# Two feed-forward layers in Strassen form: sums and low parts moved to VectorE, modulation products to ScalarE

## The reference, cut to what matters

```python
# first block, its end
x = x + rms_norm(mixed, mix_post_norm)
h = rms_norm(x, ffn_pre_norm)
f = jnp.square(jax.nn.relu(h @ w_up)) @ w_down        # 1024 -> 4096 -> 1024
x = x + rms_norm(f, ffn_post_norm)
# second block
mod = c @ w_ada + b_ada                               # 1024 -> 6 * 1024: shifts, scales, gates
...
h2 = modulate(rms_norm_2(x, g_pre_mlp), sh2, sc2)
ff = jnp.square(jax.nn.relu(h2 @ w_mlp_in)) @ w_mlp_out
x = x + gt2 * rms_norm_2(ff, g_post_mlp)
```

## Time and profile before

| | |
|---|---|
| median of three executions | 3071.1 us (3069.76 to 3072.03) |
| profiled execution, its own time | 3071.47 us |
| span of its trace, first to last instruction | 3069.7 us |
| mean granted TensorE clock | 0.953 of full speed |
| TensorE (PE) busy | 2753.1 us (90% of the span) |
| VectorE (DVE) busy | 1730.3 us (56%) |
| GpSimd (POOL) busy | 1597.4 us (52%) |
| ScalarE (ACT) busy | 1030.7 us (34%) |
| entry, up and down of run 0 | about 700 to 1523 us of the span |
| entry, up and down of run 1 | about 2280 to 3057 us |

### The profile page before, as it was taken

One profiled execution on the slowest core, in us unless ns is written; L12 is line 12 of the kernel. 1 busy time (PEld: TensorE's weight loads), 2 busy tenths in 40 slices (PEclk: granted clock), 3 DMA queues, 4 the chain that ended last, 5 costly groups with the idle time before them and its releaser, 6 DMA issues. The chain is left out here.

```text
span 3069.7 us, 39464 instructions
## 1 busy us (share of the span) xinstructions
PE 2753.1 (90%) x15794; PEld 2218.5 (72%) x15794; DVE 1730.3 (56%) x1707; ACT 1030.7 (34%) x1748; POOL 1597.4 (52%) x930
## 2 busy tenths in 40 slices
PE   7999998978899887898799999988996999978897
PEld 6887567866777666777678887656875888757775
DVE  3465544653799986776743003674144333367767
ACT  3324663325432322222420003553035333322322
POOL 4321002447688857877732322112364777678876
PEclk9999999989899998999999999999997999989999
DMA  3210000032355553223321111001133233422132
GB/s 123 55 27 16 10 1 23 3 117 96 103 185 158 184 189 116 88 75 110 110 70 50 52 35 35 14 8 49 48 138 117 76 110 110 175 100 88 62 110 110
DMA packets 219188, 256.80 MB, mean 84 GB/s; under 512 B 16119, under 2 KB 157710, under 8 KB 219022
## 3 DMA queue, kind: packets, MB, share of 16 engines
q1 hardware_dynamic: 206494, 210.97, 21.1%
q10 hardware_dynamic: 12528, 43.52, 3.7%
HBM read 204.13 MB, written 50.33 MB: 83 GB/s over the span
## 5 line engine op out<-in xcount | busy, mean ns | idle before, releaser
L369 POOL TENSOR_SCALAR slab_hi<-raw 128x1024 fp32r<-128x1024 f32 (+2 forms) x108 | 115.4, 1068 | 673.8 <-PE ps L1245 267.6
L1724 PE MATMUL ps<-down_t_lo,down_ops_rows 128*128 128x512 f32 x896 | 358.7, 400 | 0.0
L1671 PE MATMUL ps<-act_hi,up_hi 128*128 128x512 f32 (+1 forms) x544 | 213.4, 392 | 46.2 <-DVE up_hid L3002 30.5
L372 POOL TENSOR_TENSOR slab_lo<-raw,slab_hi 128x1024 fp32r<-128x1024 f32 (+2 forms) x108 | 249.3, 2309 | 9.0
L1723 PE MATMUL ps<-down_t_hi,down_ops_rows 128*128 128x512 f32 x448 | 181.3, 405 | 69.1 <-POOL down_t_lo L1136 47.2
L1136 POOL TENSOR_TENSOR down_t_lo<-down_b,down_ops_rows 128x1024 fp32r<-128x1024 f32 x56 | 174.9, 3144 | 108.8 <-ACT down_ops_rows L2368 108.8
L1723 PE MATMUL ps<-down_ops_rows 128*128 128x512 f32 x448 | 180.5, 403 | 45.6 <-POOL down_t_lo L1136 32.4
L1136 POOL TENSOR_TENSOR down_t_lo<-down_b,down_t_hi 128x1024 fp32r<-128x1024 f32 x56 | 174.5, 3136 | 83.8 <-ACT down_t_hi L2368 83.8
L1672 PE MATMUL ps<-act_lo,up_hi 128*128 128x512 f32 (+1 forms) x544 | 211.1, 388 | 0.0
L1673 PE MATMUL ps<-act_hi,up_lo 128*128 128x512 f32 (+1 forms) x544 | 210.8, 388 | 0.0
L1147 POOL TENSOR_TENSOR down_b<-down_b,down_b 128x2048 f32<-128x2048 f32 x32 | 192.7, 6023 | 22.8 <-DMA hid_spill<-up_hid 19.0
(11 more groups left out here) (375 smaller groups left out, 7272.9 us busy)
## 6 DMA issues: line engine op xcount, KB each, us to landing
hid_spill<-up_hid ACTq DMA_DIRECT2D x30, 1024.0 KB, 7.1
raw<-in_w_in SPq DMA_DIRECT2D x56, 512.0 KB, 3.8
w_ada<-in_w_ada SPq DMA_DIRECT2D x48, 512.0 KB, 3.9
down_rows<-hid_spill SPq DMA_DIRECT2D x24, 1024.0 KB, 5.0
raw<-in_w_out SPq DMA_DIRECT2D x32, 512.0 KB, 3.7
up_raw<-in_w_up SPq DMA_DIRECT2D x16, 1024.0 KB, 8.7
down_b<-in_w_down SPq DMA_DIRECT2D x16, 1024.0 KB, 7.4
up_raw<-in_w_mlp_in SPq DMA_DIRECT2D x16, 1024.0 KB, 5.7
```

Source lines behind the costliest of these rows:

```text
L372: pool.tensor_tensor(self.lo[s][:, 0:width], self.raw[r][:, 0:width], self.hi[s][:, 0:width].bitcast(F32), ALU.subtract).then_inc(self.spl ...
L1671: pe.matmul(out, up_hi[slot][:, k, :], hi, start=(p in (1, 2, 5) and k == 0), stop=False, skip_group_check=True)
L1724: pe.matmul(out, ops["s_hi"][:, k, cols], ops["t_lo"][:, k, :], start=False, stop=False, skip_group_check=True)
```

## The change

- **Up:** all low parts and all four sums move from GpSimd to VectorE (`up_low`, `up_add`), ordered product by product in one loop over `UP_ORDER`.
- **Modulation:** the multiplication by `c` moves to ScalarE, as eight instructions of 128 x 128 for each tile (`scale_ada`), spread one tile at a time over the products 1, 5, 2 and 7 of a step (`ada_step_tile`); `ADA_SHARE` becomes 3, 4, 3, 4, ..., 3, 3 over steps 1 to 14, so that none is left in step 15.
- **Last step:** products run 1, (4, 3 of step 14), 5, 2, 3, 6, 7, 4. Product 3 gets a PSUM bank of its own; 6, 7 and 4 follow each other in one bank.
- **Down:** both low parts and all eight sums on VectorE, in single instructions of 128 x 2048 (`prepare`); takes in pairs, 128 x 1024 (`down_take`, t = 0 and 2). The operands have new places: the first blocks can be loaded and split while the last up products still run (after product 3 of step 15), and for chunks 1 to 3 the loads of the next chunk start by product e = 2, 4, 5, 6.
- **Entry:** the second half of the turned activations is read before the weights are split (`t_values` 4 to 7 before `up_hi` 1 and 5); the turns stand after token tile 1 of m = 12 and 0 of m = 13 in the projection; GpSimd splits projection slabs 12 and 13 between the norms; VectorE makes the early products' weight sums and low parts inside `t_prep`; in ScalarE's queue the copy of the first early product stands ahead of `up_hi` 3; the store of the early results goes behind three of the high parts.
- Loads of the next stage (SP) start when 23 of the 28 low parts of `t` are done, in place of the end of the down products.

The core of the diff:

```diff
+UP_LAST = (5, 2, 3, 6, 7, 4)
-ADA_SHARE = [3] * (FFN_STEPS - 5) + [4, 4, 4, 3]
+ADA_SHARE = [3, 4] * 6 + [3, 3]
...
-        down_rows = sb("down_rows", 89, [P, 16, SEQ])
...
+        down_ops = [{kind: sb(f"down_{kind}{s}", 89 + 32 * s + 8 * n, [P, 4, HALF], F32R)[:] for n, kind in enumerate(("s_hi", "s_lo", "t_hi", "t_lo"))}
+                    for s in range(2)]
...
-                for n in (12, 21, 22):
-                    a_load(0, n)
+                a_load(0, 11)
+                sp.wait_ge(sem("up_prod"), FROM["up_prod"] + n0 + UP_AT[last, 2] + 1)
+                a_load(0, 12)
+                sp.wait_ge(sem("up_prod"), FROM["up_prod"] + n0 + UP_AT[last, 6] + 1)
+                b_load(0, 21)
+                sp.wait_ge(sem("up_prod"), FROM["up_prod"] + n0 + UP_AT[last, 7] + 1)
+                a_load(0, 21)
+                b_load(0, 12)
+                a_load(0, 22)
+                b_load(0, 22)
...
+                            if i == 0 and t == 1:
+                                pe.wait_ge(sem("up_out"), FROM["up_out"] + 3 * FFN_STEPS * run + OUT_AT[last, 3])
+                            elif i == 0 and t == 3:
+                                pe.wait_ge(sem("up_copied"), FROM["up_copied"] + 4 * FFN_STEPS * (run + 1))
...
-                                pe.wait_ge(sem("down_taken"), FROM["down_taken"] + 4 * (i0 + before) + t + 1)
+                                pe.wait_ge(sem("down_taken"), FROM["down_taken"] + 2 * (i0 + before) + t // 2 + 1)
...
+            def scale_ada(n):
+                act.wait_ge(sem(f"ada_in{n % 2}"), 16 * (n // 2 + 1))
+                for k in range(KD):
+                    ins = act.activation(ada[n % 2][:, k, :], ada[n % 2][:, k, :], ACT.Copy, scale=vec2[:, N_BADA + k:N_BADA + k + 1])
+                ins.then_inc(sem("ada_scaled"), 1)
...
+                for n, (u, p) in enumerate(UP_ORDER):
+                    if (u, p) == (last, 7):
+                        down_lo(run, 0)
+                    for x in up_outs(n - 1):
+                        output(*x)
+                    for x in up_adds(n + 7):
+                        up_add(run, ring, *x)
+                    if n == 0 or n >= 3 and n + 5 < UP_TOTAL:
+                        up_low(run, *UP_ORDER[n + 5])
+                    if run == 0:
+                        for m in ada_step_tile(*UP_ORDER[n - 1]) if n else ():
+                            modulation(m)
...
+                def prepare(i):
+                    c, e = i // 7, i % 7
+                    if e == 0 and c:
+                        down_s(run, c, 1)
+                        down_t(run, c, 1)
+                    elif e == 2:
+                        down_s(run, c, 4)
+                    elif e == 3:
+                        down_s(run, c, 3)
+                        down_t(run, c, 3)
+                    elif e == 4:
+                        down_t(run, c, 4)
+                    if i + 1 == DOWN_TOTAL:
+                        return
+                    down_lo(run, i + 1, "s")
+                    if e == 1:
+                        down_s(run, c, 2)
+                    down_lo(run, i + 1, "t")
+                    if e == 1:
+                        down_t(run, c, 2)
+                    if i == 0:
+                        dve.wait_ge(sem("up_prod"), FROM["up_prod"] + UP_TOTAL * (run + 1))
+                        down_s(run, c, 1)
+                        hid_stored(dve, run, FFN_STEPS - 1)
+                        down_t(run, c, 1)
...
-                for t in range(4):
+                for t in (0, 2):
                     ffn_finish(run, tag, row, t)
+                    ffn_finish(run, tag, row, t + 1)
                     down_take(run, last + 5, t)
```

More of the change, by code:

```diff
@@ L74, in up_order @@
     order = [(0, p) for p in UP_FIRST]
-    for u in range(1, FFN_STEPS + 1):
-        if u < FFN_STEPS:
-            order.append((u, 1))
-        order += [(u - 1, 4), (u - 1, 3)]
-        if u < FFN_STEPS:
-            order += [(u, p) for p in UP_FIRST[1:]]
+    for u in range(1, FFN_STEPS):
+        order += [(u, 1), (u - 1, 4), (u - 1, 3)]
+        order += [(u, p) for p in (UP_FIRST[1:] if u < FFN_STEPS - 1 else UP_LAST)]
     return order
@@ L2295, in out_projection @@
                 norm_scale(pre, 7)
+                t_values(run, pre, 1, range(KD), scale, bias)
+                for p in (1, 5, 6):
+                    t_hi_part(run, pre, 1, p)
                 act.wait_ge(sem("early_squared"), FROM["early_squared"] + run + 1)
@@ L2945, in early_out, with late_and_early @@
                 dve.scalar_tensor_tensor(h, h, 0.0, h, ALU.max, ALU.mult).then_inc(sem("early_hid"), 1)
-            def late_and_early(run, pre, tag, row, ready):
-                late = list(LATE)
-                post_norm(tag, row, late[:2], ready)
+            def late_and_early(run, pre, tag, row, ring, count):
+                for t in EARLY:
+                    post_here(tag, row, t, count)
+                t_prep(run, pre, 0, ring)
+                post_here(tag, row, 4, count)
+                post_here(tag, row, 5, count)
+                up_add(run, ring, 0, 4)
+                up_low(run, 0, 4)
+                post_here(tag, row, 6, count)
+                up_low(run, 0, 3)
+                post_here(tag, row, 7, count)
                 early_out(run, 2)
-                post_norm(tag, row, late[2:], ready)
                 early_out(run, 5)
@@ L3020, in down_lo @@
[L3020 to L3032 removed]
+                    square(u, p, h)
```

443 lines of the change are left out of this document (203 added, 240 removed).

## The result

The kernel after takes 2910.8 us (median of 4 runs, 2906.2 to 2916.4) where the kernel before takes 3070.4 us in the runs beside it: a ratio of 0.948, with a 95% interval of 0.9462 to 0.9498. The forecast was 2903 us, in a range of 2882 to 2945. One execution of the kernel before beside e9 to e12 took 5487 us; the ratios of those runs leave it out. The profiled execution has an own time of 2912.2 us and a span of 2910.3; against the 3071.47 us of before that is 159.3 us less, where the sum had 168.3.

The account below looks back on a forecast made before the run. VectorE and GpSimd were taken to lengthen each other's work and hold up TensorE, busy 90%. Terms 54.7 + 57.5 + 33.3 - 1.7 + 6.5 + 18 = 168.3 us off 3071.47 gave 2903 us, range 2882 to 2945.

Parts of the forecast that it names:

- 0.5 us per chunk before e = 1: Down, regular chunks: VectorE's first take comes at 11.2 to 11.3 us, needed at 10.88, so TensorE idles about 0.5 us.
- the new excess: Down: time over its products falls from 66.4 and 69.2 us to 11.7, gaining 54.7 in run 0, 57.5 in run 1.
- the working of chunk 0: Down's first chunk: the sum of t waits for step 15's store; product 1 starts 2.5 us late, plus about 1 low clock.
- The end: Down, before its last product: two ffn_finish stand before the first take of product 26; idle 6.2 us against 5.87 before.
- The term of run 0: Up of run 0: from 347.0 us to 313.7, a gain of 33.3 us.
- The last step's two waits: Up's last step: product 7 waits 1.7 us and product 4 waits 0.8 us for copies, 2.5 us in each run.
- Run 1: Up of run 1: 2.5 us of new waits less 0.8, a loss of 1.7 us.
- Between up and down: First down product: waits of 3.52 and 2.98 us both go, as operands are split during the last up products; 6.5 us.
- Entries: Entry into up: late turn starts 10 us earlier; 9 us gained per run, 18 in all, bounds nothing to 13.50 each.
- A: Rival in up: modulation becomes ScalarE's bound or its tiles come late; the 33 us are not won, 2936 us; chance 0.12.
- B: Rival: the entry gains nothing and chunk 0 of down stays late, product 1 waiting 12 us; 2940 us; chance 0.13.
- C: Rival in down: VectorE's instructions stay long with GpSimd silent; gain lost at 3.3 us each, 3190 us at 4.4; chance 0.03.

Follow-up runs that it names:

- e9: Kernel after, with GpSimd's early norm roots all ahead of the split of tile 12 again: 2905.9 us, ratio 0.9457.
- e12: e2 with GpSimd's four sums of a chunk in the order of before, two ahead of the second low part, two ahead of the fourth: 2995.2 us, ratio 0.9749.
- e6: Kernel after, with the two takes of the first down product put ahead of the first chunk's sums on VectorE: 2895.0 us, ratio 0.9426.
- e1: Kernel after, plus three unused 128x1024 differences on GpSimd behind each of the first 21 products of down run 0: 2965.9 us, ratio 0.9658.
- e2: Kernel after, with low parts and sums of down's weight side on GpSimd again, in the order of after: 2951.7 us, ratio 0.961.
- e3: Kernel after, with low parts and sums of the weights in the main part of up on GpSimd again, both runs: 2911.0 us, ratio 0.9478.
- e4: Kernel after, with the products of modulation on VectorE again, one 128x1024 operation a tile: 2907.1 us, ratio 0.9467.
- e5: Kernel after, with both undone in up: weight low parts and sums on GpSimd, modulation products on VectorE: 2951.8 us, ratio 0.9611.
- e10: Kernel after, with down's first two data blocks and first weight block loaded only behind the last step's fourth product: 2929.3 us, ratio 0.9535.
- e8: Kernel after, with the early turns placed behind tiles 12 and 13 of the out projection again: 2905.4 us, ratio 0.9461.
- e11: Kernel after, with the modulation products done twice on ScalarE, first by 1.0, then by the vector: 2940.4 us, ratio 0.9568.

## Why the prediction held, and where it was off

**Down.** The price of VectorE's instructions was right (2.29 us, chunks of 76.9 us for 76.7), and so was 0.5 us per chunk before e = 1. (The row of 2.29 us that it calls a sum is a low part; the sums of after take 2283 ns, so nothing hangs on it.) Mis-sized was the new excess: 11.7 us were predicted, 309.3 - 293.8 = 15.5 and 17.0 are measured. The step that failed is the working of chunk 0, which was to cost 3.5 us: product 1 starts 4.5 and 5.7 us late, and the slow matmuls behind the wait, 0.63 us each for 0.39, cost 1.5 and 2.3 us more, 6.0 and 8.0 in all. The prediction's words are: "its first sum of `t` needs the last store of step 15", hence product 1 "starts 2.5 us late". In the trace the sum of `t` waits for nothing. ScalarE's relu and square and two DMA issues (one in run 1) put the high part for product 1 late, in run 0 VectorE's low part stands behind it until 1109.18 and waits 0.65 us more for a data block (2.39 us in run 1), and two low parts and two sums precede the take: 4.30 and 5.52 us. e6 shows that the place of the take is the cause: moved ahead, the wait goes. The end was predicted at 6.2 us of idle time and is 5.21 + 1.63 and 5.53 + 0.78; a regular chunk has 0.7 us over its products for 0.5.

**Why down gained.** The argument "the two engines lengthen each other's work, and together they hold up TensorE" is half of it. e1 shows the lengthening by itself. But on the way from before over e12 and e2 to after, the 51 us of a run fall into about 5 that were not divided, 22 for the order of GpSimd's queue, and 24 for taking its part away. These shares hang on the order of the steps: from e12 straight to after, the same move is worth 46 us (355.2 to 309.3), since it does away with the queue too. The forecast did not need the division, because it was counted from VectorE's queue in the kernel after, and so it came out all the same. What the prediction did not see is that more than half of the gain could be had with GpSimd still at work.

**Up.** The load of VectorE was about right: 17.3 of 20.4 us, 85%, were predicted for a step with four tiles; over the whole stage after has 233 of 307, 76%, and e4 shows 288 of 307 without a wait. So the margin was larger than thought, and the prediction did not see that the two moves replace each other: e3 and e4 each keep the whole gain, e5 loses it. The term of run 0 came out 3.9 us better than the sum. A modulation tile on TensorE was taken at 0.34 us, out of a step that also had a wait and slow matmuls behind it. In after the steps take 19.83 us with three tiles and 20.02 with four, where 20.0 and 20.4 were forecast; over the 19.04 of the products that is 0.25 us a tile, some 4 us less in all. The last step's two waits are 1.65 + 0.77 = 2.4 us for 2.5. Run 1 lost 2.9 us for 1.7. Of the 1.2 us between, 1.1 lie at its start: the first 30 matmuls take 6.34 us (2274.38 to 2280.72, granted clock 0.52, nearly all at the lower level of 1.2 GHz) against 5.27 in before (2382.13 to 2387.40, clock 0.66), both behind a wait of some 4.27 us. Why the clock rises later in after, no run shows.

**Between up and down.** Both waits are gone, as worked out. e10 shows that the early loads are needed for it, since without them a longer wait stands before product 7. It does not show that they are what removed the waits of before, which were not for loads. In run 1 TensorE waited for GpSimd's low part of `t`; in run 0 it waited for the copy of the modulation columns, which stood in ScalarE's queue behind a store that waited for VectorE's last result (timeline of ScalarE of before):

```profile
1151.23 0.20 ACT L2378 COPY mod_cols<-ps 128x48 f32<-128x48 f32 x1 [4.83 <-DVE up_hid L3004]
```

The new order of the last step and the low part on VectorE bear on both; no run undoes one of them alone.

**Entries.** 14.3 us for 18, well inside the bounds. The late turn starts at 775.17 us, 6.6 earlier for 10; the 3.28 us of idle time before the first turn were foreseen as about 3. That the earlier place of the turns helps fell with e8: it moves a wait and wins nothing. What does win, GpSimd without low parts of up or ScalarE's new order, no run here tells apart; it stays open, and in run 0 so does the size, by the spread above.

**The rivals.** A (ScalarE the bound): the short operations come every 117.6 / 384 = 0.31 us, above the 0.26 taken and inside its bounds, and ScalarE is busy 216 of 307 us; e11 shows the price beyond the margin. B: the entries did gain, and of its late blocks little came: VectorE waits 0.65 and 2.39 us for one, and chunk 0 is late by 4 to 6 us and not 12, mainly by the place of the take. C (VectorE long without GpSimd): refuted by 2.28 us throughout, and shown by e1 with GpSimd at work, where it took back all of down's gain at a mean of 3.24 us, near its point of 3.3 us.

The group of the new operations in up of run 0 of after:

```profile
L2253 ACT ACTIVATE w_ada<-w_ada,vec_cols 128x128 f32<-128x128 f32 x384 | 117.6, 389 | 3.6 <-DMA w_ada<-in_w_ada 3.5
```

## What to carry to other kernels

In these runs an operation of GpSimd on SBUF costs twice: its own time, and what it adds to VectorE's operations beside it that read two operands from SBUF. But before moving it, look at the order of its queue: here 22 of 51 us were a low part, needed at once, behind two long sums, and in the first chunk behind the wait for a store that it did not itself need. Compare an engine's work with the time that the stage takes without waits, and not its busy share, which was 94% in e4 without a wait and 93% in e5 with them. Undo the parts of a change singly and together: two moves that each look necessary can replace each other. An instruction that waits for a load, placed early in an in-order queue, makes everything behind it wait for that load, and a copy out of PSUM that frees a bank belongs ahead of sums that nobody needs yet; but behind a wait that is removed the next one may stand just as long, as at the end of down.

## What the runs showed of the hardware

Of VectorE's operations in these stages, those that slow beside GpSimd read both operands from SBUF. Those with one operand from PSUM do not: the add takes 682 ns in e3, as in after (686), and the takes 1216 ns in e1. An operation with a single operand from SBUF was not looked at. And in e3 the sums do not grow in proportion: 128 x 128, 128 x 256 and 128 x 512 grow from 292, 425 and 687 ns to 1011, 956 and 1278, by 720, 530 and 590 ns. That looks like waiting for a turn rather than a halved rate. The plainest row is a tiny product in down of run 0 of e2, which takes 200 ns in after:

```profile
L3176 DVE TENSOR_TENSOR mod_cols<-mod_cols,vec_cols 128x48 f32<-128x48 f32 x1 | 2.4, 2367 | 0.0
```

The Trainium skill says so in "SBUF — State Buffer", section "SBUF: two separate sides": the pair of ports is an exclusive lock, held for a whole instruction, and a VectorE operation with two SBUF inputs asks for it, against a GpSimd operation that reads SBUF. The rows of e3 and e2 agree with it.

A short ScalarE operation with its scale from SBUF takes 389 ns and comes every 306; with a constant as scale, in e11, 298 ns. "ScalarE: Activation LUTs" of the Trainium skill, section "What ACT_TABLE_LOAD costs", puts these at an estimated 386 and 293 ns (186 ns, 0.833 ns an element, and 93 ns for an operand that is a pointer) with an overlap of 93 ns between neighbours, so 293 ns apart; the trace agrees within 13 ns.
